# A decoder layer on eight cores: DMA semaphores, the engine that stores y, how far state-space inputs run ahead, and where q/k/v weights are loaded

## What is computed

```python
z = h @ w_in                       # q, k, v | u | gates
# B: three head groups, (window, dilation) = (128,1), (512,4), (2048,16)
outs, lses = dilated_window_attention(q, k, v, rel_bias, window, dilation)
y_attn = sum(softmax(lses) * outs)
# A: state space, 32 groups of 16 channels, 64-dim complex state per group
x_t = Abar * x_{t-1} + Bbar * u_t;  y_t = Re(C x_t) + D * u_t
y_ssm = gelu(y);  a, b = split(y_ssm @ w_glu);  y_ssm = a * sigmoid(b)
mix = (g_ssm * (y_ssm @ w_ssm_proj) + g_attn * (y_attn @ w_attn_proj)) @ w_out
h = layer_norm(ALPHA * h + mix)
h = layer_norm(ALPHA * h + (relu(h @ w_up) ** 2) @ w_down)
```

## Time and profile before

| | us |
|---|---|
| runs shown | 2303.77, 2519.8, 2321.04 |
| median | 2321.04 |
| profiled execution, its own time | 2303.47 |
| its span (slowest core, core 5) | 2301.9 |

### The profile page before, as it was taken

One profiled execution on the slowest core, in us unless ns is written; L12 is line 12 of the kernel. 1 busy time (PEld: TensorE's weight loads), 2 busy tenths in 40 slices (PEclk: granted clock), 3 DMA queues, 4 the chain that ended last, 5 costly groups with the idle time before them and its releaser, 6 DMA issues.

```text
span 2301.9 us, 31192 instructions; the slowest of 8 cores (2273.6 to 2301.9 us)
## 1 busy us (share of the span) xinstructions
PE 1948.0 (85%) x10468; PEld 949.5 (41%) x10468; DVE 950.4 (41%) x1396; ACT 704.0 (31%) x1058; POOL 296.7 (13%) x338
## 2 busy tenths in 40 slices
PE   3598665566677866999999998998998999999997
PEld 1355352332434522434444443444443443444443
DVE  6364342252323244326525534534534533533533
ACT  2365331242234472331331241242142142132120
POOL 5470111111110011010010010010000001001000
PEclk8799787777888977999999999999999999999999
DMA  9665654455576436435635625734833843642640
GB/s 176 145 213 111 128 122 112 113 120 131 120 113 120 158 126 213 130 130 172 240 100 198 242 90 193 258 110 151 292 119 133 292 138 115 249 163 110 221 146 37
DMA packets 112381, 359.72 MB, mean 156 GB/s; under 512 B 18240, under 2 KB 55488, under 8 KB 85184
## 3 DMA queue, kind: packets, MB, share of 16 engines
q1 hardware_dynamic: 88048, 273.72, 34.7%
q0 software_dynamic: 24176, 83.99, 18.1%
HBM read 356.72 MB, written 74.97 MB: 188 GB/s over the span
## 4 chain that ended last, share of the span: by engine, by line
PE 57%; DMA 23%; DVE 6%; issue 4%; SPq 4%; ACT 4%; POOL 1%; DVEq 0%; ACTq 0%; POOLq 0%
PE ps L459 56%; DMA y_scratch<-arena 7%; DMA arena<-u_scratch 6%; DVE arena L499 4%; SPq L449 4%; DMA sw_scratch<-arena 3%; DMA arena<-wb_out 2%; ACT arena L505 2%; DMA arena<-wb_dn 1%; DMA arena<-w_qkv 1%; ACT arena L471 1%; DMA tab_scratch<-arena 1%; PE ps L464 1%; ACT L471 1%; DVE arena L489 1%
## 5 line engine op out<-in xcount | busy, mean ns | idle before, releaser
L459 PE MATMUL ps<-arena 128*128 128x512 bf16 (+4 forms) x10148 | 1929.6, 353 | 278.4 <-DMA arena<-sw_scratch 138.0
L459 PEld LDWEIGHTS ps<-arena 128*128 128x128 bf16 (+2 forms) x10148 | 933.6, 106 | 1257.2 <-issue 438.2
L471 ACT ACTIVATE arena<-ps 128x512 f32<-128x512 f32 (+2 forms) x384 | 261.0, 680 | 480.0 <-PE ps L459 394.0
L489 DVE TENSOR_TENSOR arena<-ps,arena 128x512 f32<-128x512 f32 (+1 forms) x193 | 127.6, 687 | 472.1 <-PE ps L459 350.2
L489 DVE TENSOR_TENSOR arena<-arena 128x512 f32<-128x512 f32 (+6 forms) x267 | 182.1, 705 | 241.5 <-ACT arena L471 200.4
L499 DVE SCALAR_TENSOR_TENSOR arena<-ps,arena 128x512 bf16<-128x512 f32 x256 | 176.8, 691 | 245.1 <-ACT arena L471 245.0
L489 POOL TENSOR_TENSOR arena<-arena 128x512 bf16<-128x512 f32 (+1 forms) x128 | 163.0, 1276 | 863.4 <-DVE arena L489 696.6
L505 ACT CAST arena<-ps 128x512 bf16<-128x512 f32 (+1 forms) x217 | 121.1, 569 | 268.3 <-PE ps L459 227.6
L471 ACT ACTIVATE arena<-arena 128x512 f32<-128x512 f32 (+6 forms) x186 | 101.2, 546 | 297.2 <-DVE arena L1087 256.4
L499 DVE SCALAR_TENSOR_TENSOR arena<-arena,ps 128x512 f32<-128x512 f32 x128 | 87.1, 685 | 252.8 <-PE ps L459 251.5
L499 DVE SCALAR_TENSOR_TENSOR arena<-arena 128x1024 f32<-128x1024 f32 (+1 forms) x131 | 167.1, 1276 | 21.5 <-ACT arena L471 5.9
(11 more groups left out here) (28 smaller groups left out, 156.1 us busy)
## 6 DMA issues: line engine op xcount, KB each, us to landing
arena<-wb_up SPq DMA_DIRECT2D x64, 1024.0 KB
arena<-wb_dn SPq DMA_DIRECT2D x64, 1024.0 KB
arena<-wb_gate SPq DMA_DIRECT2D x32, 1024.0 KB
arena<-wb_out SPq DMA_DIRECT2D x16, 1024.0 KB
arena<-x POOLq DMA_DIRECT2D x32, 512.0 KB, 6.5
out<-arena POOLq DMA_DIRECT2D x32, 512.0 KB, 5.5
arena<-sw_scratch SPq DMA_DIRECT2D x32, 288.0 KB
arena<-x_tile POOLq DMA_DIRECT2D x8, 1024.0 KB, 41.9
```

The source lines that it names most:

```text
L459: return P.add("pe", lambda e: e.matmul(out, lhsT, rhs, start=start, stop=stop, **kw), R(*reads), R(*writes), cost=c)
L471: return P.add("act", lambda e: e.activation(out, in_, func, bias=bias, scale=scale), R(*reads), R(*writes), cost=c, aset=ASETS.get(func))
L489: return P.add(eng, lambda e: e.tensor_tensor(out, in0, in1, op), R(*reads), R(*writes), cost=ew_cost(eng, out, [in0, in1], True))
```

## The change

Six edits:

1. Semaphores for DMAs: 40 on SP, 24 on POOL, 12 on ACT, in place of 12 each.
2. The two y stores of a group are issued by ACT, in place of SP.
3. State-space inputs have four buffers; four groups are loaded at the start, and `ssm_in(g + 4)` stands behind `ssm_y(g)`.
4. "prep" has five staging buffers `stg` in place of two, "tabs" three `gcs` in place of two.
5. Three `wq` buffers: the first round's three pieces are loaded by POOL next to the first tile of x; each next round's piece is loaded as soon as the piece of this round is used.
6. The planner's model: one queue for the DMAs of SP and ACT, 70 ns to issue, 2100 ns to land, and 120 bytes per ns on it while POOL's queue is busy.

```diff
+    NDMA = {"sp": 40, "pool": 24, "act": 12, "pe": 0, "dve": 0}
...
-        dma_free = {"pool": 0.0, "sp": 0.0, "act": 0.0}
+        dma_free = {"pool": 0.0, "hw": 0.0}
...
-                issue = 1000.0 if e == "pool" else 120.0
+                issue = 1000.0 if e == "pool" else 70.0
                 free[e] = t + issue
+                q = "pool" if e == "pool" else "hw"
                 rate = 140.0 if e == "pool" else 280.0
-                dma_free[e] = max(dma_free[e], t + issue) + op.nbytes / rate
-                op.fin = dma_free[e] + 1900.0
+                if q == "hw" and dma_free["pool"] > t:
+                    rate = 120.0
+                dma_free[q] = max(dma_free[q], t + issue) + op.nbytes / rate
+                op.fin = dma_free[q] + 2100.0
...
-    wq = [ar.alloc([8, 128], BF16) for _ in range(2)]
+    wq = [ar.alloc([8, 128], BF16) for _ in range(3)]
...
             for ft in range(1, 4):
                 dma("pool", wu[ft].ap, wu_d[ft], [], [wu[ft]])
+            for j in range(3):
+                dma("pool", wq[j].ap, wqkv_d[0, :, j * 8:(j + 1) * 8, :], [], [wq[j]])
...
-    gcs = [ar.alloc([2, 2, 256], F32) for _ in range(2)]
+    gcs = [ar.alloc([2, 2, 256], F32) for _ in range(3)]
...
-    WSfs = [f4(), f4()]
-    bigAs, bigBs = [f4(), f4()], [f4(), f4()]
-    stg = [ar.alloc([GB, 640], BF16) for _ in range(2)]
+    bigAs, bigBs = [f4(), f4()], [f4(), f4()]
+    stg = [ar.alloc([GB, 640], BF16) for _ in range(3)]
+    ar.seek(T2, c32.span[0])
+    WSfs = [f4(), f4()]
+    stg += [ar.alloc([GB, 640], BF16) for _ in range(2)]
...
+    NS = 4
+    tabb = [ar.alloc([2, 256], F32) for _ in range(NS)]
+    swb = [ar.alloc([1152], BF16) for _ in range(NS)]
+    ugb = [ar.alloc([2, 256], BF16) for _ in range(NS)]
...
         for t in range(2):
-            dma("sp", y_d[g, :, t * 8:t * 8 + 8].rearrange("h t c -> t h c"), ysg.ap[:, t, :], [ysg], [y_res.res[g]])
-
-    ssm_in(0)
-    ssm_in(1)
+            dma("act", y_d[g, :, t * 8:t * 8 + 8].rearrange("h t c -> t h c"), ysg.ap[:, t, :], [ysg], [y_res.res[g]])
+
+    for g in range(NS):
+        ssm_in(g)
     ssm_z(0)
     for g in range(32):
         ssm_scan(g)
-        if g + 2 < 32:
-            ssm_in(g + 2)
         ssm_y(g)
+        if g + NS < 32:
+            ssm_in(g + NS)
         if g + 1 < 32:
             ssm_z(g + 1)
...
-        pieces = [wq_load(0), wq_load(1)]
         for which, dst in ((0, qT), (1, kT)):
-            w = pieces[which]
+            w = wq[which]
...
-            if which == 0:
-                pieces.append(wq_load(2))
-        w = pieces[2]
+            if rnd < 5:
+                dma("pool", w.ap, wqkv_d[rnd + 1, :, which * 8:(which + 1) * 8, :], [], [w])
+        w = wq[2]
...
+        if rnd < 5:
+            dma("pool", w.ap, wqkv_d[rnd + 1, :, 16:24, :], [], [w])
```

More of the change, by code:

```diff
@@ L189, in schedule, with finalize @@
         return max(o.fin for o in self.all)
-    def finalize(self, nc, es, ndma=12):
+    def finalize(self, nc, es):
         for e in self.ENGS:
@@ L198, in finalize @@
                 if op.dma:
-                    if len(dsems) < ndma:
+                    if len(dsems) < self.NDMA[e]:
                         dsems.append([es.enter_context(nc.semaphore(f"d_{e}_{len(dsems)}")), 0])
-                    slot = dsems[dcnt % ndma]
+                    slot = dsems[dcnt % self.NDMA[e]]
                     dcnt += 1
@@ L516, in build_program @@
     P.at("const", 0)
-    ar.seek(0, 6 * KB)
+    ar.seek(0, 8 * KB)
     smP = ar.alloc([SP_N], F32)
@@ L544, in build_program @@
     stt(f16p.ap, e_b.ap, 0.0, e_b.ap, ALU.is_lt, ALU.add, [e_b], [f16p])
-    X0, Q0, A0, E0 = 6 * KB, 70 * KB, 127 * KB, 159 * KB
-    wq = [ar.alloc([8, 128], BF16) for _ in range(2)]
+    X0, Q0, A0, E0 = 8 * KB, 72 * KB, 129 * KB, 161 * KB
+    wq = [ar.alloc([8, 128], BF16) for _ in range(3)]
     ar.seek(X0, Q0)
@@ L640, in build_program @@
     b2, c1, tx, Xb, Yb = [ar.alloc([32, 16], F32) for _ in range(5)]
+    T2 = ar.off
     ar.seek(T1)
@@ L692, in build_program @@
         g0 = gb * GB
-        st, WSf = stg[gb % 2], WSfs[gb % 2]
+        st, WSf = stg[gb % len(stg)], WSfs[gb % 2]
         (wA, wB), (lA, lB) = outer_pair(gb)
@@ L770, in build_program @@
     ar.seek(E0)
-    tabb = [ar.alloc([2, 256], F32) for _ in range(3)]
-    swb = [ar.alloc([1152], BF16) for _ in range(3)]
-    ugb = [ar.alloc([2, 256], BF16) for _ in range(3)]
+    NS = 4
+    tabb = [ar.alloc([2, 256], F32) for _ in range(NS)]
+    swb = [ar.alloc([1152], BF16) for _ in range(NS)]
+    ugb = [ar.alloc([2, 256], BF16) for _ in range(NS)]
     t12 = ar.alloc([2, 256], F32)
@@ L781, in ssm_in @@
     def ssm_in(g):
-        tb, sw, ug = tabb[g % 3], swb[g % 3], ugb[g % 3]
+        tb, sw, ug = tabb[g % NS], swb[g % NS], ugb[g % NS]
         ft, h0 = g // 8, (g % 8) * 16
@@ L790, in ssm_z @@
     def ssm_z(g):
-        sw, ug, bk = swb[g % 3], ugb[g % 3], banks[6]
+        sw, ug, bk = swb[g % NS], ugb[g % NS], banks[6]
         for z in range(2):
@@ L798, in ssm_scan @@
     def ssm_scan(g):
-        tb = tabb[g % 3]
+        tb = tabb[g % NS]
         tt("dve", t12.ap, banks[6].ap.rearrange("p (z c) -> p z c", z=2), tb.ap, ALU.mult, [banks[6], tb], [t12])
@@ L807, in ssm_y @@
     def ssm_y(g):
-        sw, ug, ysg = swb[g % 3], ugb[g % 3], ysb[g % 2]
+        sw, ug, ysg = swb[g % NS], ugb[g % NS], ysb[g % 2]
         bk = banks[7]
@@ L866, in build_program @@
         ebr = eb[rnd % 2]
-        def wq_load(which):
-            nonlocal wqi
-            w = wq[wqi % 2]
-            wqi += 1
-            dma("pool", w.ap, wqkv_d[rnd, :, which * 8:(which + 1) * 8, :], [], [w])
-            return w
-        pieces = [wq_load(0), wq_load(1)]
         for which, dst in ((0, qT), (1, kT)):
-            w = pieces[which]
+            w = wq[which]
             for t in range(8):
```

## The result

The changed kernel takes 2216.7 us (2208.4 to 2216.9). In some executions of every kernel the cores of one die show a lower clock and the time is longer (here once, 2282.5 us), so all times and ratios from here on are of the other executions. Against the kernel before the ratio is 0.957, with a 95% interval of 0.948 to 0.967: faster by some 4%, 87 us between the two profiled executions and 98 us by the ratio, where the forecast was 154 us (2150). The time lies in the stated range, 2085 to 2245; the way was right and the size was not.

The account below looks back on a forecast made before the run. SP, waiting for landings of y and u in the state-space loop, was taken as the bound. Terms 140 + 10 + 4 = 154 us off 2303.47 gave 2150 us; the range holding 8 in 10 was 2085 to 2245.

Parts of the forecast that it names:

- Semaphores: 0: All DMA queues: more semaphores gain 0 us, since SP's waits are those of second writers of one resource.
- y stores on ACT: 140 us: State-space loop: SP loses two issues and a 5.2 us wait; turn falls from 14.03 to 9.5 us, saving 140 us.
- ACT's bounds of 8.0 to 10.6: Loop turn in us set by ACT: 8.0 if other work fills 2.6 us of the landing wait, 10.6 if none.
- the time saved in the loop comes back in the attention behind it: Stated sign of being wrong: the stretch after the loop grows by what the loop saved.
- The wait for u: 3.3 to 5.2 us: SP's queue in the loop: wait for u's first load grows, bounded by 3.3 and 5.2 us a turn.
- ACT's wait: Loop: the y store's landing wait moves to ACT, partly filled with other work; waits under 3 us each.
- Four inputs ahead: Loop: SP runs up to four turns ahead, so late landings no longer stop PE; no gain beyond the turn's.
- q/k/v weights: 10 us, bounds 0 to 15: After the loop: earlier loads remove PE's two waits for w_qkv, 9.8 us; whole edit 0 to 15 us.
- Staging: plus 4 us, bounds -8 to 20: First stage: more staging and table buffers end DVE's 13.1 us stop, but SP's store chain limits the gain to 4 us.
- The planner's figures: 0: Planner's DMA model: new figures only change the fixed orders; 0 us, plus or minus 15.
- only issue time: Rival, chance 0.08: loop transfers slow as fast as asked; only 37 us of issues saved, plus 14: 2252 us.
- ACT as the bound: Rival, chance 0.16: ACT's unfilled waits make loop turns 10.6 to 13 us; at 12, total 2226 us.

Follow-up runs that it names:

- x4: Kernel before, with the halves of each y store and u load naming separate resources, so neither second half waits; orders planned anew: 2212.4 us, 0.961.
- x11: Kernel before, with the halves of y and u on separate resources but every engine's instruction order kept as before: 2203.5 us, 0.959.
- x1: Changed kernel with 12 DMA semaphores each on SP, POOL and ACT again: 2210.0 us, 0.959.
- x2: Changed kernel with the two y stores of a group issued by SP again: 2258.3 us, 0.980.
- x5: Kernel before with only the two y stores of a group moved to ACT: 2244.5 us, 0.977.
- x7: Changed kernel with q/k/v weights loaded when their round begins, through two buffers, as before: 2235.1 us, 0.973.
- x14: Kernel before with y stores on ACT and the planner's new DMA figures: 2232.2 us, 0.971.
- x3: Changed kernel with the three first-stage stores of a batch to sw_scratch on separate resources, so none waits for another: 2180.8 us, 0.947.
- x9: Changed kernel with separate resources for the halves of y and u and a batch's three sw_scratch stores, y on ACT: 2145.3 us, 0.932.
- x10: Changed kernel with y halves, u halves and sw_scratch stores all on separate resources, and y stores issued by SP: 2140.4 us, 0.931.
- x13: Changed kernel with three input buffers for the state-space groups in place of four: 2197.0 us, 0.961.
- x6: Changed kernel with two staging and two table buffers in its first stage again: 2184.1 us, 0.950.
- x8: Changed kernel planned with the DMA figures of the kernel before: 2238.0 us, 0.974.

## Why the prediction was right and wrong

**The bound.** Right. SP stood for landings of first halves; taking these waits away alone (x4, x11) is worth 4%.

**Semaphores: 0.** Right (x1).

**y stores on ACT: 140 us.** Wrong, and this is most of the miss: 48 us in the changed kernel (x2), some 54 alone (x5). The mechanism held: the wait left SP, and ACT stood for less of it. The step that failed is the product, 31 x (14.03 - 9.5). It counts a shorter turn as time gained, and that holds only if the turn still carries the same matmuls, as it does in x11. The planner makes every order anew; with the stores on ACT it put 488 matmuls fewer into the loop, and they had to be done behind it. That the turn alone came out at 9.86 us, near the 9.5, is luck, then: in loops with this wait on ACT that carried as much work as before or more it was 11.05 to 11.74 (x7, x14, the changed kernel, x1, x3), above ACT's bounds of 8.0 to 10.6. (What it would be with y on ACT and the order held, no run shows.) The forecast had named the sign itself, "the time saved in the loop comes back in the attention behind it": in x5 that stretch is 58 us longer (229.0 to 287.4). PE's idle in the loop's stage, 445 - 280.6 = 164 us, was the ceiling of what such an edit can bring, but for what a higher clock gives back, and 140 us asked for nearly all of it. Alone the edit took 57 us of that idle. My turn of 9.5 us, with 8.9 us of PE's work in it, had left PE almost none; no run here, x9 and x10 among them, came below 64 us in the loop on its slowest core (x9: 301.0 less 237.4), or below 52 on any core.

**The wait for u: 3.3 to 5.2 us.** Too low: 5.8 us with this edit alone (x5), 7.1 in the changed kernel, 21.3 at the longest. The reason was right: with y on ACT the load of u stands directly behind the weights and tables on SP's queue, as the y store did, and takes over its long wait. The upper bound took that store's wait of 5.2 us from a loop that asked for less: the DMA engines are busy 67% in x5's loop and 71 in the changed kernel's, where they were 53. It cost little, since with four groups ahead PE hardly waits for SP.

**ACT's wait.** Right in kind: 2.2 us a turn of standing, a little under the 2.6 that 8.0 us a turn allowed for, and PE's largest wait is now for ACT. But "under 3 us each" was wrong: 11 waits of 6.3.

**Four inputs ahead.** Priced in the turn as a cover; nothing to measure (x13).

**q/k/v weights: 10 us, bounds 0 to 15.** 18 to 25 us in the changed kernel (x7), 30 to 35 by the ratios. I priced PE's wait in one place. What more the loads bring shows as 246 matmuls more in the loop; why the planned order puts them there isn't shown.

**Staging: plus 4 us, bounds -8 to 20.** Wrong in sign: minus 16 to 33 (x6). I had named the right next thing, SP's chain of stores, but held it to end where it did before, at 208.1 us; the loop starts 48 us later. That lateness isn't the staging's: with two buffers the start is still 261.2 us, and in x14 the planner's figures alone, on top of y on ACT, bring it.

**The planner's figures: 0.** Wrong: 21 to 28 us (x8), 33 to 37 by the ratios. "They only change the fixed orders" was true and no reason for nothing, with engines that wait for each other's place in these orders. The last stage, at least, is where I had it: unchanged.

**The sum.** Undone one at a time and set against x1, the edits account for 48 + 25 + 28 - 26 = 75 us by the times and 48 + 30 + 33 - 20 = 91 by the ratios, of 90 to 94. With intervals of 4 to 16 us on each, these runs don't show whether anything is left for how the edits act together. That the time lies in the stated range, with four of its terms mis-sized, is in part luck: the figures' and the weights' unforeseen gain stands in for a part of what the stores didn't bring. The rivals: "only issue time" gave 2252 us, near what the stores alone brought (2244.5), but for a reason that x10 contradicts: there the two issues are back on SP and cost nothing. "ACT as the bound" gave 2226 us, nearest to the measured time, with turns above 10.6 and ACT standing before its second store; both are so in the changed kernel, but the loop there carries 318 matmuls more, so its turn is no test of that sum.

## What to carry to other kernels

Where a planner orders the work anew, price an edit by the idle time that it takes from the engine all the work must pass (here PE, medians over the cores: 266 us ahead of M before, 205 after, 146 at best) and by what a higher clock takes off its busy time (607, 564, 548), not by how much shorter one loop becomes: the loop's work moves. Look for waits that the program's own bookkeeping makes (two halves of one tensor under one name) before moving them to another engine: freeing those of y and u alone (x4, x11) gave what all six edits gave, and freeing all on top of the edits (x9, x10) 60 to 75 us more. And when buffers are added ahead of a serial queue, follow that queue to its end.

## What was not expected of the hardware

SP waited 7.1 us in the mean for a load of 64 KB (u) to land, in place of 3.3. Not all of this goes with the DMA engines' share, which went from 53 to 71%: the load's place on SP's queue changed too. Where SP stores y (the kernel before, x2), the y store (128 KB) stands directly behind 544 KB of weights and tables and is waited for 5.2 and 5.7 us; the load of u, behind the y stores, 3.3 and 4.1. Where ACT stores y, the load of u has the place behind the weights and tables: 5.8 us in x5 (67% busy), 7.1 in the changed kernel, x14 and x3 (71 to 74%). How much each of the two adds isn't separated. In x9 and x10 they were busy 86 and 87% in the loop and PE's idle still fell, so shares of that size left room. DMAs issued by ACT showed as a queue of their own (q10), beside SP's q1.
